# Latent attention decode: keys turned by DVE in blocks of 32, scores on sixteen tiles of the array

## What is computed

```
def mla_sample(q_nope, q_rope, latent, k_rope, lat_past, kr_past, w_uk, w_uv):
    q_lat = einsum('bqhd,rhd->bqhr', q_nope, w_uk)          # 8 heads, rank r = 256
    s_past = (einsum('bqhr,bkr->bhqk', q_lat, lat_past)
              + einsum('bqhd,bkd->bhqk', q_rope, kr_past)) * SM_SCALE   # d = 32
    p = softmax(concat([s_past, s_new]))
    o_lat = einsum('bhqk,bkr->bqhr', p[..., :n_past], lat_past) + ...
    return einsum('bqhr,rhd->bqhd', o_lat, w_uv)
lat_past = cache_latent[page_table]     # (8, 8192, 256), pages of 128 tokens
kr_past = cache_k_rope[page_table]      # (8, 8192, 32)
```

## Time and profile before

| | us |
|---|---|
| runs, lowest, median, highest | 2019.30, 2026.57, 2026.62 |
| the profiled execution's own time | 2019.72 |
| its span, first to last instruction | 2017.9 |
| busy in the span: PE, weight loads, DVE, ACT, POOL | 1763.9, 1574.5, 862.7, 562.5, 201.3 |
| mean granted clock of TensorE | 0.915 |

### The profile page before, as it was taken

The page is one execution under the profiler, slowest core; times in us unless marked ns, Lnnn a source line. Parts: engine busy times, 40 slices in busy tenths (PEclk is TensorE's granted clock), DMA queues, the critical chain, the costliest instruction groups (busy, mean ns, idle before and its releaser), DMA issues. The chain is left out here.

```text
span 2017.9 us, 31568 instructions
## 1 busy us (share of the span) xinstructions
PE 1763.9 (87%) x12773; PEld 1574.5 (78%) x12773; DVE 862.7 (43%) x1657; ACT 562.5 (28%) x1025; POOL 201.3 (10%) x174
## 2 busy tenths in 40 slices
PE   5889999849799788988879829999999999999981
PEld 2467777629799666666759829999999999999981
DVE  1234444473343544454532863433343334333437
ACT  1134444342211243534443332111211111111123
POOL 1032222020000202020202320000000000000006
PEclk8899999959899878878789959999999999999995
DMA  9697767150111100000023222111211121212013
GB/s 362 235 395 262 275 258 266 51 162 19 51 43 42 32 0 14 1 13 0 0 78 100 75 81 67 50 45 31 62 37 57 31 62 31 62 31 62 1 49 140
DMA packets 116489, 183.39 MB, mean 91 GB/s; under 512 B 17038, under 2 KB 86358, under 8 KB 112300
## 3 DMA queue, kind: packets, MB, share of 16 engines
q1 hardware_dynamic: 106428, 101.71, 16.0%
q0 software_dynamic: 8192, 75.85, 9.9%
q10 hardware_dynamic: 1776, 4.51, 0.6%
HBM read 172.06 MB, written 9.94 MB: 90 GB/s over the span
## 5 line engine op out<-in xcount | busy, mean ns | idle before, releaser
L1951 PE MATMUL ps<-mix_conv,wf_hl 128*128 128x384 f32 (+1 forms) x1584 | 272.4, 321 | 11.3 <-DVE wf_hl L1976 11.3
L1951 PE MATMUL ps<-mix_attn,wf_hl 128*128 128x384 f32 (+1 forms) x1584 | 271.0, 319 | 0.0
L1951 PEld LDWEIGHTS ps<-mix_conv,wf_hl 128*128 128x128 f32 x1584 | 255.1, 189 | 11.4 <-DVE wf_hl L1976 11.4
L1951 PEld LDWEIGHTS ps<-mix_attn,wf_hl 128*128 128x128 f32 x1584 | 253.7, 188 | 0.0
L1965 PE MATMUL ps<-hid,wd_hl 128*128 128x384 f32 (+1 forms) x1584 | 249.9, 318 | 0.0
L1965 PEld LDWEIGHTS ps<-hid,wd_hl 128*128 128x128 f32 x1584 | 248.8, 188 | 0.0
L1991 DVE TENSOR_TENSOR h<-ps,gate 128x384 f32<-128x384 f32 (+1 forms) x66 | 34.0, 516 | 320.3 <-PE ps L1951 320.3
L2006 DVE TENSOR_TENSOR acc<-ps,acc 128x384 f32<-128x384 f32 (+1 forms) x240 | 123.8, 516 | 93.4 <-PE ps L1965 93.4
L1022 PE MATMUL ps<-U,wc_hl 128*128 128x384 f32 (+1 forms) x864 | 138.3, 323 | 8.7 <-DVE wc_hl L1036 8.7
L1022 PEld LDWEIGHTS ps<-U,wc_hl 128*128 128x128 f32 x864 | 138.1, 191 | 9.0 <-DVE wc_hl L1036 9.0
L473 PE MATMUL ps<-ident,lat_raw 128*128 128x128 f32 x1024 | 125.7, 276 | 12.0 <-DMA lat_raw<-in_cache_latent,idx 11.5
(11 more groups left out here) (313 smaller groups left out, 2497.1 us busy)
## 6 DMA issues: line engine op xcount, KB each, us to landing
w_ada_sb<-in_w_ada SPq DMA_DIRECT2D x12, 2048.0 KB, 19.6
wf_raw<-in_w_gate SPq DMA_DIRECT2D x22, 512.0 KB, 4.0
wf_raw<-in_w_up SPq DMA_DIRECT2D x22, 512.0 KB, 5.3
wd_raw<-in_w_down SPq DMA_DIRECT2D x22, 512.0 KB, 5.8
wc_raw<-in_w_in SPq DMA_DIRECT2D x24, 256.0 KB, 3.1
x_nat<-in_x_prompt SPq DMA_DIRECT2D x4, 1024.0 KB, 8.3
wo_raw<-in_w_o SPq DMA_DIRECT2D x8, 512.0 KB, 4.0
ln_x<-in_x_prompt SPq DMA_DIRECT2D x8, 512.0 KB, 4.4
```

The source lines that it names most:

```text
L1951: last = pe.matmul(ps[:, 2 * (q % 2) + g, 0:tn], a, x, start=j == 0, stop=j == 3 * KD - 1)
```

## The change

In the decode loop the latents and rotary keys are no longer turned by PE. DVE turns them from SBUF to SBUF with its own transpose, which turns each block of 32 x 32 by itself: four instructions of 128 x 1024 for the latents of a group and one of 128 x 512 for its rotary keys. A turned block of 32 partitions holds 32 components of the keys of 32 rows. The score product is therefore cut into products with 32 rows: for each of 8 blocks b of the latent rank, for each of four parts a of the partitions and four parts c of the tokens, one product with 32 x 32 weights and 128 moving columns; a picks the rows of the array and the PSUM bank (0 to 3), c its columns and the 32 partitions of the result. The rotary keys add 16 such products. That is 144 products a group in place of 24. Scores now fill 128 columns of each of four banks instead of one bank of 512, in a single set where there were two. ACT copies the turned probabilities, which DVE did. q32 must hold the query's blocks on each part of the partitions: in the first stage PE makes four more products with selecting matrices (`q_pick`, made by DVE at the start), and DVE copies them out.

```
# first stage
+ dve.tensor_copy(q_pick[:].rearrange("p b (a d) -> p b a d", a=4), ident[...] broadcast over a)
# PE, after piece 10
+ pe.wait_ge(dve1, V["q_lat"])
+ for b in range(4):
+     last = pe.matmul(ps[:, 7, b * P:(b + 1) * P], q_pick[:, b, :], q_lat[:], start=True, stop=True)
# DVE
+ dve.tensor_copy(q_lat[:], ps[:, 6, 0:P]).then_inc(dve1, 1)
+ mod(9)
+ dve.wait_ge(pe1, E["q_blocks"])
  for k in range(KV):
+     src = ps[:, 7, :].rearrange("p (b k h s) -> p k s b h", b=4, k=KV, h=H)[:, k]
+     order.mark(dve.tensor_copy(q32[:, :, 4 * k:4 * k + 4, 0:H], src))

# decode, PE
- def turn_lat(g, j): ...
- def turn_kr(g): ...
  def score(g):
      s = g // GPS
+     pe.wait_ge(turned, g + 1)
+     wait(pe, exp_out, g)
+     for b in range(8):
+         for a in range(4):
+             rows = slice(32 * a, 32 * a + 32)
+             for c in range(4):
+                 pe.matmul(ps[32 * c:32 * c + 32, a, 0:P], q32[rows, s, b, :],
+                           latT[rows, g % 2, 4 * c:4 * c + 4, b, :], start=b == 0, stop=False)
+     for a in range(4):
+         rows = slice(32 * a, 32 * a + 32)
+         for c in range(4):
+             last = pe.matmul(ps[32 * c:32 * c + 32, a, 0:P], zk[rows, s, :],
+                              krT[rows, g % 2, 4 * c:4 * c + 4, :], start=False, stop=True)
  for t in range(NGR + 2):
+     score(t - 1); weigh(t - 2); turn_p(t - 1)

# decode, ACT: rows(t, 0), rows(t, 2) and the copy of krT are gone
+ act.activation(p_sb[:].rearrange("p i a n -> p a i n"), ps[:, 0:4, 0:P]..., ACT.Exp, ...)
  act.activation(o_all[...], ps[:, PO, 0:KVR], ACT.Copy)
+ act.activation(pT[:, g % 2, :, :, 0:H], ps[:, PTURN, :]..., ACT.Copy).then_inc(pT_out, 1)

# decode, DVE
+ def turn(g, c):
+     at = slice(4 * c, 4 * c + 4)
+     dve.transpose(latT[:, g % 2, at]..., raw[:, g % RAW, at]...)
  for t in range(SLOTS):
      if t < NGR:
+         dve.wait_ge(lat_in[t % RAW], 16 * (t // RAW + 1))
+         wait(dve, scored, t - 1)
+         turn(t, 0); turn(t, 1)
      g = t - 1
      if 0 <= g < NGR:
          dve.wait_ge(scored, g + 1)
+         dve.tensor_reduce(m, ps[:, 0:4, 0:P], mybir.AxisListType.XY, ALU.max)
          dve.tensor_scalar(negm[...], m, -1.0, None, ALU.mult)
      if t < NGR:
+         turn(t, 2); turn(t, 3)
+         dve.wait_ge(kr_in[t % RAW], 16 * (t // RAW + 1))
+         dve.transpose(krT[:, t % 2]..., kraw[:, t % RAW]...).then_inc(turned, 1)
      # merge as before
```

More of the change, by code:

```diff
@@ L142, in phase_modulation_and_sample_projection @@
         prod = sb("prod_s", [NS, H, HD])
+        q_lat = sb("q_lat", [P, P])
+        q_pick = sb("q_pick", [P, 4, P])
         c_in, b_in, x_in, wn_in, wu_in, small_in = (sem(n) for n in (
@@ L296, in _ @@
                         last.then_inc(pe1, 1)
+                    if n == 10:
+                        pe.wait_ge(dve1, V["q_lat"])
+                        for b in range(4):
+                            last = pe.matmul(ps[:, 7, b * P:(b + 1) * P],
+                                             q_pick[:, b, :], q_lat[:],
+                                             start=True, stop=True)
+                        last.then_inc(pe1, 1)
                 turn(11)
@@ L468, in _ @@
             def _(pe):
[L469 to L483, removed]
@@ L485, in score @@
                 def score(g):
                     s = g // GPS
[L487 to L494, removed]
@@ L502, in turn_p @@
                     pe.wait_ge(exp_out, g + 1)
+                    wait(pe, pT_out, g)
                     for i in range(4):
-                        last = pe.transpose(ps[:, PSC[g % 2], i * P:(i + 1) * P], p_sb[:, i * P:(i + 1) * P], ident[:])
+                        last = pe.transpose(ps[:, PTURN, i * P:(i + 1) * P], p_sb[:, i].rearrange("p a n -> p (a n)"), ident[:])
                     last.then_inc(p_turned, 1)
@@ L591, in _ @@
                     if t < NGR:
-                        rows(t, 3)
-                    if 0 <= g < NGR:
-                        dve.wait_ge(p_turned, g + 1)
-                        wait(dve, weighed, g - 1)
-                        dve.tensor_copy(pT[:, g % 2, :, :, 0:H],
-                                        ps[:, PSC[g % 2], :].rearrange("p (i j h) -> p i j h", i=4, j=4)[:, :, :, 0:H])\
-                           .then_inc(pT_out, 1)
+                        turn(t, 2)
+                        turn(t, 3)
+                        dve.wait_ge(kr_in[t % RAW], 16 * (t // RAW + 1))
+                        dve.transpose(krT[:, t % 2].rearrange("p i n -> p (i n)"),
+                                      kraw[:, t % RAW].rearrange("p i d -> p (i d)")).then_inc(turned, 1)
                     if t % GPS == 1 and t > GPS:
```

84 lines of the change are left out of this document (34 added, 50 removed).

## The result

The changed kernel takes 2157.93 us in the median of four runs (2157.06 to 2166.43), the kernel before 2026.12 us (2019.3 to 2026.62): a ratio of **1.067, 95% interval 1.063 to 1.070**. The prediction said 1964 us and faster; the time lies above its range too. The profiled execution has a span of 2155.7 us, so 137.8 us more than before.

A forecast was written before the change was run, and what follows sets the result against it. PE was taken to bound the decode stage. With DVE the new bound, the stage was to fall from 293.7 to 235 us (-58.6) and the first stage to grow by 1.3: 1963, stated as 1964 us, range 1947 to 2013.

The forecast's parts named there:

- PE's total: Decode loop: PE's score, weighing, turn of probabilities and tile changes sum to 4.4 us a slot, no longer the bound.
- Can loads start fast enough for 16 tiles: Decode score on PE: loads 7 ns apart, from eight loads of L493, just enough for 0.11 us.
- the predicted slot of 7.1 us: Decode loop: DVE's transposes, maximum, negative, semaphores and merge sum to 7.1 us a slot, making DVE the bound.
- DVE: Decode loop: a transpose of 1024 columns takes 1.22 us, like one-element-a-cycle operations; ends 0.75 and 2.45 us.
- D: Rival, decode loop: DVE turns 4-byte blocks at half rate, 2.45 us each; total 2139 us; chance 0.08.
- The score: Decode loop, PE: the score's 288 pairs take 2.0 us, 2.2 us until another engine knows.
- run 18 rounds in 2.0 us: Decode score on PE: sixteen tiles side by side need 288 / 16 = 18 rounds of 0.11 us, 2.0 us.
- S + 4.2: Decode slot if DVE waits for the score; S is the score's time to its notice; 9.0 us at S 4.8.
- Rival C: Decode score: 32 x 32 tiles issue no faster than 25 ns a pair; slot 11.6, total 2107 us; chance 0.09.
- Rival B: Decode score: row groups run two at a time, 36 rounds; slot 8.4, total 2004 us; chance 0.14.
- Rival E: Decode loop: PE, partly idle, runs at 1.2 GHz; slot some 8.6, total 2012 us; chance 0.06.
- The first stage: First stage: eight more pairs on PE ahead of the modulation's last pieces add 1.3 us, ends 0.9 and 2.0.

The follow-up runs named there:

- diagonal: The changed kernel with one score product over 128 rows, queries block-diagonal, in place of four over 32: 1960.02 us, 0.969 of the kernel before.
- experiment 6: The diagonal kernel with 100 tiny products a pass added on PE: 2171.59 us; with only the first six groups gathered as well: 2094.48 us.
- no_gather: The changed kernel with only the first six groups of cache rows gathered and used again by later ones: 2078.03 us.

## Why the prediction was wrong

**The step that failed** is PE's total, "= 4.4 us a slot: no longer the bound", and ahead of it "Can loads start fast enough for 16 tiles ... It is just enough". That sum counted PE in columns of the array and checked a rate over eight loads. It had no term for where the instructions come from. In the place of "no longer the bound" the runs put the instruction packets: 648 / 256 = 2.53 a slot, and the slot of 12.7 us is 5.0 us for each of them, where the predicted slot of 7.1 us left 2.8. The page of before had the row for it, the instruction queue with 68 packets in 2018 us, which no step of the prediction read: nobody waited for it at 240 instructions in 8.97 us. The count of instructions, 240 before and 648 after, stood in the prediction as 120 pairs that it never added up and 288 that it used for columns alone.

Point by point:
- **DVE**: right. 1.22 was predicted for a transpose, 1.215 measured. D (2.45) is excluded, and the estimate of 7.1 us a slot was high by 0.6 once DVE was the bound, in the diagonal kernel, whose maximum runs over 128 and not 512 columns: that alone saves 0.4 us (0.25 to 0.29 us in place of 0.69).
- **The score**: mis-sized even without stops. 2.0 us were predicted from 7 ns a load. The bursts measured 12.8 ns a pair, so 288 pairs take 288 x 12.8 = 3.7 us. The error was to take the spacing of eight loads on four tiles for the spacing of pairs on sixteen: the start of pairs is fast enough (8.0 ns with the tiny products of experiment 6), but the sixteen tiles do not run 18 rounds in 2.0 us. By the prediction's own rules, slot = S + 4.2 = 3.9 + 4.2 = 8.1 us and stage = 5.6 + 31 x 8.1 + 3.9 + 7.3 = 268 us, an estimate: without its stops the change would have won some 24 us, not 57.
- **Rival C** had the sign and the place (the maximum waits for the score: 181.5 us), but a time 51 us too short (2107), and not the cause. Its 25 ns a pair do not occur: 12.8 ns are under the 16 ns from which it decided. It would have led to a wrong cure, larger tiles, while experiment 6 shows the larger tiles just as slow once the instructions are as many.
- **Rival B** (row groups two at a time, 36 rounds) fits the score within its bursts. It gave 4.0 us for the products, 3.7 were measured; 32 pairs in 0.40 to 0.42 us are four rounds of 0.10 to 0.105 us, where full overlap would need two. The diagonal kernel supports it: 72 pairs on four column tiles, 18 rounds, take some 2.0 us (from the first multiplication of L491 at 317.79 to the first weighing at 319.78, and the same 1.99 us in 14 of the 31 scores), about half of the score on 32 x 32 tiles. The size is B's; that row groups wait for each other is not shown, since no run varies them alone. B was not what made the kernel slower: its 2004 us leaves out the stops.
- **Rival E**, the clock: present (0.78, weighing products at twice their length), but it falls after the stops, as the windows above show. In diagonal it is 0.93.
- **The first stage**: +1.3 predicted, 2.0 measured. The eight added multiplications took 2.05 us at a granted clock of 0.50, where the sum had at most twice 8 x 0.11.

By the Trainium skill (Runtime: NRT & Kernel Launch, "Instruction fetch mechanics") instructions come in blocks of 16 KiB, 256 of them, the next block fetched while the current one runs, and this is hidden because the sequencer dispatches more slowly than the fetch fills. The first half agrees with 16.4 KB a packet and with stops at multiples of 256, and the second with the kernel before, where 240 instructions in 8.97 us met no stop. The traces contradict the second half for a stretch in which PE takes an instruction each 6.4 ns: 256 are gone in 1.6 us, and PE then stands for up to 5.1.

The packet records also show what a packet costs in time without the gather's traffic (10.2 us a slot, 4.0 for each packet). In 27 of the 38 stops of no_gather from 150 to 400 us the next packet starts 1.0 to 1.3 us after PE goes on; it takes some 1.1 us, and PE goes on some 1.4 us after it has landed. That makes 3.5 us, and no two packets of that run start less than 3.3 us apart. With the gather the packet itself is no longer (1.0 us in the median), but only 17 of the 44 start that early, the others 1.6 to 6.5 us after PE goes on. So it is the start of the packet that the gather delays. Two packets of this queue never overlap.

What stays open: what the 1.4 us between landing and going on are, why the score's bursts take 12.8 ns a pair, and how the loss divides between the stops themselves (126.9 us by the count above) and the clock that they halve. Loops that run the same instructions again in this stage, or a gather cut into smaller pieces so that instruction packets find a gap, were not tried.

## What to carry to other kernels

Count instructions as you count columns: where a change makes many small ones out of few large ones, divide the instructions that an engine issues in a slot by 256 and set the slot against it. Here, with 2.5 packets a slot, a slot took some 5.0 us for each packet beside the gather and 4.0 us without it (each packet more or less changed it by 4.1 us beside the gather). In a profile the sign is a bottleneck engine that stands idle in a wait without a name (`issue`), at whole multiples of 256 instructions, beside a growing `instruction` queue; the cure is the same work in fewer instructions, even if most of a weight tile is zeros.

## What the hardware showed that I had not expected

- PE stops at borders of 256 instructions: 40 of 44 stops over 0.9 us, up to 5.1 us each with the gather, up to 2.4 without it. Traffic on data queues slows down an engine's own program (79.5 us of the span).
- PE goes on 1.1 to 1.6 us after an instruction packet has landed (43 of 44 stops).
- PE took pairs of load and multiplication 8.0 ns apart when the products had 8 columns, and 12.8 ns apart on sixteen tiles of 32 x 32 with 128 columns.
- A no-operation on PE costs 74 ns by its own records (75 to 78 by the spans), in proportion to its number, and isn't the neutral filler that it seems.
- DVE's transpose in blocks of 32 takes 1.215 us for 128 x 1024 fp32, as long as a plain copy of that size (1.22).
